# A hybrid decoder layer: the S5 output powers moved from VectorE to GpSimd, and the S5 chunk work moved ahead of two column panels

## The reference

```python
def s5_mixer(u, a_re, a_im, log_dt, b_re, b_im, c_re, c_im, d_skip, w_glu):
    ug = u.astype(f32).reshape(B, L, S5_GROUPS, S5_GROUP)          # 16 groups of 16 channels
    A_bar = jnp.exp(dt * A)                                        # 64 complex states for each group
    B_bar = ((A_bar - 1.0) / A)[..., None] * B_c
    bu = jnp.einsum('blgc,gpc->blgp', ug, B_bar)
    _, states = lax.associative_scan(combine, (a_seq, bu), axis=1)
    y = jnp.real(jnp.einsum('blgp,gcp->blgc', states, C_c)) + d_skip * ug
    y = jax.nn.gelu(y.reshape(B, L, S5_WIDTH))
    return y * jax.nn.sigmoid(y @ w_glu)
```

## Time and profile before

| | |
|---|---|
| median of 3 runs | 1481.87 us (1480.95 to 1482.01) |
| the profiled execution | 1483.24 us, its span 1481.5 us |
| granted TensorE clock, mean | 0.977 of 2.4 GHz |
| busy: PE, PE weight load | 1416.6 us (96%), 1158.4 us (78%) |
| busy: DVE, ACT, POOL | 680.3 us (46%), 354.0 us (24%), 473.1 us (32%) |
| chain that ended last, by engine | PE 86%, DVE 9%, ACT 3%, issue 1% |

### The profile page before, as it was taken

The page is one execution under the profiler, slowest core; times in us unless marked ns, Lnnn a source line. Parts: engine busy times, 40 slices in busy tenths (PEclk is TensorE's granted clock), DMA queues, the critical chain, the costliest instruction groups (busy, mean ns, idle before and its releaser), DMA issues.

```text
span 1481.5 us, 18380 instructions
## 1 busy us (share of the span) xinstructions
PE 1416.6 (96%) x7437; PEld 1158.4 (78%) x7437; DVE 680.3 (46%) x1053; ACT 354.0 (24%) x621; POOL 473.1 (32%) x240
## 2 busy tenths in 40 slices
PE   5997799999999899999999999999999999999998
PEld 4886467799887767777788888788888888888887
DVE  5898665535452553444345331533222232464641
ACT  5311544400101133444411010421111111232110
POOL 4333002234723110111034433234343343444542
PEclk9998899999988899999999999999999999999999
DMA  7420101032101010000011141411111111141122
GB/s 182 45 52 19 43 1 29 15 77 54 37 19 52 1 36 1 19 18 19 1 36 54 36 163 43 156 44 43 57 42 56 44 43 56 42 168 46 43 74 97
DMA packets 126821, 76.44 MB, mean 52 GB/s; under 512 B 39312, under 2 KB 113424, under 8 KB 126736
## 3 DMA queue, kind: packets, MB, share of 16 engines
q1 hardware_dynamic: 126752, 75.46, 18.2%
HBM read 66.93 MB, written 8.52 MB: 51 GB/s over the span
## 4 chain that ended last, share of the span: by engine, by line
PE 86%; DVE 9%; ACT 3%; issue 1%; DMA 0%; SPq 0%; ACTq 0%; DVEq 0%
PE ps L642 23%; PE ps L643 22%; PE ps L644 22%; PE ps L1125 4%; PE ps L1155 3%; PE ps L1139 2%; PE ps L877 1%; PE ps L894 1%; PE ps L907 1%; PE ps L657 1%; PE ps L1083 1%; DVE merged L1708 1%; DVE arena L1523 1%; PE ps L1102 1%; PE ps L851 1%
## 5 line engine op out<-in xcount | busy, mean ns | idle before, releaser
L554 POOL TENSOR_TENSOR wh<-raw,zero 128x1024 fp32r<-128x1024 f32 (+2 forms) x93 | 189.0, 2032 | 975.7 <-PE ps L644 957.8
L642 PE MATMUL ps<-hTh,wh 128*128 128x512 f32 x1008 | 404.2, 401 | 3.9 <-ACT arena L1346 3.1
L643 PE MATMUL ps<-hTl,wh 128*128 128x512 f32 x1008 | 397.3, 394 | 0.0
L644 PE MATMUL ps<-hTh,wl 128*128 128x512 f32 x1008 | 397.1, 394 | 0.0
L557 POOL TENSOR_TENSOR wl<-raw,wh 128x1024 fp32r<-128x1024 f32 (+2 forms) x93 | 257.9, 2773 | 7.3
L642 PEld LDWEIGHTS ps<-hTh,wh 128*128 128x128 f32 x1008 | 192.7, 191 | 44.0 <-ACT arena L1346 3.5
L644 PEld LDWEIGHTS ps<-hTh,wl 128*128 128x128 f32 x1008 | 192.2, 191 | 41.2
L643 PEld LDWEIGHTS ps<-hTl,wh 128*128 128x128 f32 x1008 | 192.6, 191 | 38.0
L644 PE MATMUL ps<-wh,hTl 128*128 128x512 f32 (+2 forms) x512 | 179.1, 350 | 0.0
L642 PE MATMUL ps<-wh,hTh 128*128 128x512 f32 (+2 forms) x512 | 179.0, 350 | 0.0
L643 PE MATMUL ps<-wl,hTh 128*128 128x512 f32 (+2 forms) x512 | 179.0, 350 | 0.0
(11 more groups left out here) (331 smaller groups left out, 1598.9 us busy)
## 6 DMA issues: line engine op xcount, KB each, us to landing
raw<-in_w_in SPq DMA_DIRECT2D x35, 512.0 KB, 3.9
raw<-in_w_up SPq DMA_DIRECT2D x32, 512.0 KB, 4.1
raw<-in_w_down SPq DMA_DIRECT2D x16, 512.0 KB, 3.7
merged<-in_x SPq DMA_DIRECT2D x8, 512.0 KB, 7.3
raw<-in_w_out SPq DMA_DIRECT2D x8, 512.0 KB, 3.7
merged<-in_x SPq DMA_DIRECT2D x2, 2048.0 KB, 10.1
x_keep<-merged SPq DMA_DIRECT2D x2, 2048.0 KB, 10.4
conv<-x_keep SPq DMA_DIRECT2D x1, 2048.0 KB, 8.3
```

The costliest lines, as they stand in the source:

```text
L554: eng.tensor_tensor(wh[:, p, 0:n], raw[:, p, 0:n], zero1[:, 0:1].broadcast_to((P, n)), ALU.add).then_inc(s_hi[0], 1)
L642: mm(out_, ah, bh, start=first, stop=False, skip_group_check=True)
L643: mm(out_, ah, bl, start=False, stop=False, skip_group_check=True)
L644: return mm(out_, al, bh, start=False, stop=last, skip_group_check=True)
```

## The change

GpSimd gets a function `output_powers`, called between the splits of panels 5 and 6. It computes `c_pow` with the same six tensor_tensors that VectorE had, with its temporaries in the region of `u_chunk` instead of `mixT`. It waits for a new semaphore `c_own_ready`, and for the group transposes, which read `u_chunk`. VectorE loses the six, and waits for `c_pow` once, ahead of the attention loop. TensorE runs `lag_kernels`, `w_transposes` and `chunk_inputs` ahead of `proj(4)`, and ScalarE's evacuations 8 and 9 (of `proj(4)`) go behind those of the lag kernels and of the transposed input weights.

```diff
@@ GpSimd
+            def output_powers():
+                full = (P, 8, 8, 16)
+                tmp = [s5w[:, 1024 * i:1024 * i + 1024].rearrange("p (i m c) -> p i m c", i=8, m=8) for i in range(2)]
+                pb = [x.unsqueeze(3).broadcast_to(full) for x in p_nat]
+                vb = [x.rearrange("p (i c) -> p i c", i=8).unsqueeze(2).broadcast_to(full) for x in c_own]
+                eng.wait_ge(S("c_own_ready"), 1)
+                eng.wait_ge(S("ug_ps"), 4)
+                for k, op in enumerate((ALU.add, ALU.subtract)):
+                    eng.tensor_tensor(tmp[0], pb[0], vb[k], ALU.mult)
+                    then(eng.tensor_tensor(tmp[1], pb[1], vb[1 - k], ALU.mult))
+                    ins = eng.tensor_tensor(c_pow[k], tmp[0], tmp[1], op)
+                    if k == 0:
+                        then(ins)
+                ins.then_inc(S("c_pow"), 1)
+
             for p in range(3, P_NSAPROJ + 9):
+                if p == 6:
+                    output_powers()
                 split_panel(p)
@@ TensorE
                     if m == 8:
-                        eng.wait_ge(S("cT_read"), 2)
+                        eng.wait_ge(S("lag_read"), 1)
...
             def lag_kernels():
                 eng.wait_ge(S("e_ready"), 1)
-                eng.wait_ge(S("main_free"), 9)
+                eng.wait_ge(S("cT_read"), 2)
...
             grp_transposes()
-            proj(4)
             lag_kernels()
             w_transposes()
             chunk_inputs()
+            proj(4)
             proj(5)
@@ ScalarE
-            evac(8)
-            evac(9)
             eng.wait_ge(S("lag_ps"), 1)
...
-            for m in range(10, 16):
+            for m in range(8, 16):
                 evac(m)
@@ VectorE
...
+            ins.then_inc(S("c_own_ready"), 1)
...
-            powers(c_pow, p_nat, c_own, (ALU.add, ALU.subtract)).then_inc(S("c_pow"), 1)
-            eng.wait_ge(S("c_pow"), 1)
...
             eng.wait_ge(S("consts"), 1)
+            eng.wait_ge(S("c_pow"), 1)
```

More of the change, by code:

```diff
@@ L1675, in _ @@
                     r = slice(64 * g, 64 * g + 64)
-                    eng.tensor_copy(c_own[ri][r].rearrange("p (i c) -> p i c", c=16),
-                                    cT[ri][r].rearrange("p (i g c) -> p i g c", g=2, c=16)[:, :, g, :])
+                    ins = eng.tensor_copy(c_own[ri][r].rearrange("p (i c) -> p i c", c=16),
+                                          cT[ri][r].rearrange("p (i g c) -> p i g c", g=2, c=16)[:, :, g, :])
+            ins.then_inc(S("c_own_ready"), 1)
             for k in range(9):
```

## The result

| | before | changed |
|---|---|---|
| median | 1482.03 us | 1487.90 us (six runs each) |
| ratio of the two | | 1.0036, 95% interval 1.0023 to 1.0049 |
| the profiled execution | 1483.24 us, span 1481.5 | 1488.5 us, span 1486.8 |

The change makes the kernel 5.9 us slower by the medians, 5.3 by the ratio (3.4 to 7.3). The forecast was +8.1, 1490.0. One execution of a later kernel (the powers alone), in a slow state at 2836 us, is left out; all others here are fast ones.

The account below looks back on a forecast made before the run. VectorE's S5 chain bounds the kernel: from 81.5, 37.3 us of work plus 30.9 of blocks end L1721 at 149.7 against 140.9, 8.8 later; less 0.7 gives +8.1, 1490.0 us from 1481.87. Range 1484.5 to 1496.

Parts of the forecast that it names:

- The bound: VectorE's serial S5 work, through L1721, ends TensorE's 9.56 us gap at 141.74 us; its shift reaches the end unchanged.
- main step: From 81.6 us GpSimd's six powers make VectorE's two-input SBUF instructions stand: 14.4 us of blocking against 7.3 us saved.
- The price of the six: The six output powers on GpSimd at 2.4 us each, 14.4 us in all; the ends are 11.4 and 16.6.
- the 0.7 that I had taken off: Short VectorE instructions slip in at each of GpSimd's 14 starts, some 0.05 us each, shortening VectorE's delay.
- The splits: GpSimd's splits 6 to 9 block VectorE's chain for 4.3, 2.3, 5.2 and 4.7 us.
- TensorE's lateness: TensorE reaches the attention 7.7 us later, at 139.2: 5.2 from the new order, 2.5 from low clock behind its gap.
- its cover: TensorE still arrives ahead of VectorE, so none of its 7.7 us reaches the end.
- Rival (a): The exclusion spares the six, or VectorE wins its turns; TensorE binds: -3.4 us, 1478.5, chance 0.08.
- the 1.6 us from there to `sb_z(1)`: In (a), TensorE goes from `sb_z(0)` at 139.2 to 140.8: 0.7 for matmuls and mask, 0.9 for ScalarE.
- the 2.5 us of clock: In (a), the gap before `sb_z(1)` that held the clock at half for 5 us is gone, saving 2.5 us.
- Rival (b): Alignment eats the cost: the six near 1.9 us each, split 9 misses the scans; +0.4 us, 1482.3, chance 0.13.
- (c): Repeated operands are slow on GpSimd, over 3.3 us each: +13.5 us, 1495.4; at 5 us each +24; chance 0.09.

Follow-up runs that it names:

- the powers alone: Kernel before with only the six output powers moved to GpSimd, TensorE's and ScalarE's order as before; 1.0039, +5.8 us.
- memset kernel: Changed kernel with the six output powers replaced by seven GpSimd memsets of 2,048 elements, so c_pow is zero; 1.0023, +3.4 us against the kernel before.
- filled changed kernel: Changed kernel with 22 extra unused matmuls of 512 columns before TensorE's wait for e_ready; 1.0010, +1.5 us against the kernel before.
- order-only kernel: Kernel before with only TensorE's and ScalarE's new order, the output powers left on VectorE; 1.0023, +3.4 us.
- memset kernel of the old order: Seven GpSimd memsets in place of the six output powers, TensorE's and ScalarE's order as before the change; 0.9947, -7.9 us against the kernel before.
- both filled kernels: 22 unused matmuls before TensorE's wait for e_ready, in the new order: powers on VectorE 1.0008, +1.2 us; powers on GpSimd 1.0010, +1.5 us.
- kernel before with later splits: Kernel before with GpSimd's splits of panels 8 and 9 waiting until TensorE is in the GLU matmuls; 0.9953, -7.0 us.
- the powers last: Kernel before with the six powers on VectorE behind both chunk_states, TensorE's wait for c_pow behind the Toeplitz matmuls; 0.9966, -5.0 us.

## Why the prediction was right, and where it was off

**The bound and the main step held.** VectorE's serial S5 work ended the gap, the six output powers on GpSimd stopped it, and the kernel became slower. These two engines thus meet at more than semaphores, other than the opening has it. The memset kernel shows that GpSimd's writing does not exclude VectorE's two-input instructions, which leaves its reading; "SBUF — State Buffer" of the Trainium skill, section "Who interferes with whom", makes that distinction too, and the trace agrees: 0.16 us beside memsets, 1.9 beside multiplies.

**The price of the six was mis-sized.** Four multiplies took 1.93 us and only the two adds 2.35: 12.4 us, not 14.4. The ones with repeated operands were the faster; that the repetition did it, and not the multiply, was not tested by itself, but L554, an add with a repeated operand, takes 1.93 as well. Of the 12.4, VectorE lost 11.0 (16.0 less 5.0), since a short instruction got through at most handovers. At `sb_z(1)` the change is worth 6.4 less the late start of 0.8, 5.6 us, against 8.1 forecast; 14.4 counted for 11.0 lost, less the 0.7 that I had taken off, is 2.7 too much; the splits cost 0.3 more than forecast, and with that the difference is accounted for. The estimate from the Trainium skill's "GPSIMD Engine Reference", section 3.1, 2.25 us each, is near the adds alone (2.35 in this trace) and above the multiplies (1.93).

**The splits came out near the sum, not one by one.** From long less normal durations the four cost 3.8, 3.8, 4.4 and 4.8 us, 16.8; the forecast had 4.3, 2.3, 5.2 and 4.7, 16.5. Split 7 met the scans instead of the PSUM-reading instructions, because VectorE's table was ready sooner than forecast (113.3 for about 118) and TensorE came later; split 9 met the end of `chunk_states(1)` instead of its scans. With 37.3 us of work the end comes out at 82.3 + 37.3 + 11.0 + 16.8 = 147.4; measured 147.2. That the four came out at the forecast's sum is luck: in the filled changed kernel they cost 13.0.

**TensorE's lateness was put too small, and its cover thinner than stated.** I had 7.7 us, 2.5 of it for the low clock; the profile of the changed kernel has 9.5 (10.3 less the late start of 0.8), the others in the new order without filler up to 12. The gap was near the forecast (4.86 for 5.1 us); what was mis-sized is the clock: lag kernels, transposes and chunk inputs took 14.4 us (81.47 to 95.90) instead of 9.9. Bound by TensorE, `sb_z(1)` would have come at 141.78 + 2.86 = 144.6 there, 3.5 us before VectorE let it; with the arrival of the order-only kernel it would have been 147.1, 1 us before. The order change by itself costs 3.4 us. The forecast held because the two costs lie side by side, and by a margin of 1 to 3.5 us where I had counted on 9.

**Rival (a) was priced with the wrong sign.** Without the exclusion the kernel would not have been 3.4 us faster but, by the memset kernel, 3.4 slower. The steps of (a) that failed are TensorE's arrival at 139.2 (there 143.3), the 1.6 us from there to `sb_z(1)` (2.87), and the 2.5 us of clock that were to come back behind the shorter gap: from `sb_z(1)` to the end of the Toeplitz matmuls only 0.8 did. So faster was not to be had from this change in any case. Rival (b) was not met: split 9 fell on L1734 and L1735. (c) is excluded by 1.93 us each.

## What to carry to other kernels

Work moved from VectorE to GpSimd is not off VectorE as long as both read SBUF with two inputs: price it at GpSimd's full duration against what VectorE saves, here 12.4 us on GpSimd, of which VectorE lost 11.0, against 7.3 saved. Look first for GpSimd work that already runs beside VectorE's critical stretch and can wait: two splits moved later brought 7.0 us here, about what taking the powers off VectorE at no cost would have (7.9, in the memset kernel of the old order). And before reordering TensorE to start something early, ask who waits for it, and what the gap in front of it does to the clock and to every transfer and split that follows TensorE.

## What the runs showed of the hardware that I had not expected

A GpSimd tensor_tensor of 1,024 fp32 elements took 1.93 us with both operands repeated (multiply) and 2.35 us with two plain ones (add or subtract). GpSimd memsets of 2,048 elements, back to back for 13 us, left VectorE's two-input instructions at 0.16 us.

Behind a gap of 4.9 us TensorE's clock fell to 1.2 GHz. It was back after 10 to 11 us in the two profiles of the changed kernel, and after about 15 in four others of the new order, while TensorE ran the lag kernels, the transposes and part of the chunk inputs; behind the gap that ended at 141.74 it was back after about 5. In both filled kernels, without the gap, the stretches from 80 to 98 us have a granted clock of 1.00. But in the kernel before with later splits it fell in the old order, with no gap in front. Its stretches, columns as in the earlier trace rows:

```profile
80.00:86.00 6.00, 6.00 (x28) 4.97 (x27) 5.49 (x33) 0.60 (x1) 0.33 (x1) 1.00 0.02 4
86.00:92.00 6.00, 6.00 (x44) 5.77 (x43) 5.70 (x18) 0.98 (x2) 4.28 (x2) 0.88 0.00 0
92.00:98.00 6.00, 5.31 (x67) 5.08 (x67) 5.67 (x30) 2.39 (x4) 0.00 (x0) 0.83 0.19 22
```

TensorE was busy throughout the first two, and at `sb_z(0)` it was 2.2 us later than before, 0.7 of it from the start. The profile with the powers last has the same (0.95 and 0.77 from 86 to 98 us). Which executions get the long spell was not settled.
